# Routed experts of a mixer and MoE layer: gate and up products made transposed, weight loads split in two

## The reference

```python
def moe_ffn(h, w_router, router_bias, wg, wu, wd, sg, su, sd):
    xf = h.reshape(-1, d).astype(F32)
    idx, w = route(xf, w_router, router_bias)          # 6 of 64 experts for each token
    routed = routed_experts(xf, idx, w, wg, wu, wd)
    shared = (silu(xf @ sg) * (xf @ su)) @ sd
    return (routed + shared).reshape(bsz, seq, d)
# for the rows x of one expert e, each with its weight:
#   y = (silu(x @ wg[e]) * (x @ wu[e])) @ wd[e],   wg, wu: 1024 x 256,   wd: 256 x 1024
```

## Time and profile before

| what | us |
|---|---|
| runs (three) | 2062.09, 2062.33, 2065.42 |
| median | 2062.33 |
| profiled execution, span from first to last instruction | 2064.1 |
| of it: TensorE busy | 1995.9 |
| VectorE, GpSimd, ScalarE busy | 1138.1, 774.3, 504.3 |

### The profile page before, as it was taken

The page is one execution under the profiler, slowest core; times in us unless marked ns, Lnnn a source line. Parts: engine busy times, 40 slices in busy tenths (PEclk is TensorE's granted clock), DMA queues, the critical chain, the costliest instruction groups (busy, mean ns, idle before and its releaser), DMA issues.

```text
span 2064.1 us, 23702 instructions
## 1 busy us (share of the span) xinstructions
PE 1995.9 (97%) x7237; PEld 1014.8 (49%) x7238; DVE 1138.1 (55%) x3065; ACT 504.3 (24%) x1102; POOL 774.3 (38%) x717
## 2 busy tenths in 40 slices
PE   8999999999999999999999999999999999999991
PEld 6444667575544444444445554444444444444440
DVE  6222546776611222335676656966666666666645
ACT  3111554452322222214432230111111111111113
POOL 1762005612122222115980002554545545545531
PEclk9999999999999999999999999999999999999996
DMA  5421000011132222144253006999999999999974
GB/s 147 132 87 41 21 21 22 22 47 47 46 130 75 72 82 77 57 124 167 101 203 144 38 31 258 341 356 348 349 356 352 358 361 350 352 352 354 353 238 168
DMA packets 129639, 370.45 MB, mean 179 GB/s; under 512 B 33712, under 2 KB 65668, under 8 KB 103832
## 3 DMA queue, kind: packets, MB, share of 16 engines
q1 hardware_dynamic: 103960, 314.83, 40.8%
q0 software_dynamic: 23520, 54.61, 10.9%
q10 hardware_dynamic: 2080, 0.01, 0.1%
HBM read 320.57 MB, written 68.17 MB: 188 GB/s over the span
## 4 chain that ended last, share of the span: by engine, by line
PE 46%; POOL 3%; DVE 2%; issue 2%; DMA 1%; ACT 0%; SPq 0%; DVEq 0%; POOLq 0%
PE banks L3164 22%; PE banks L3180 10%; PE banks L2288 4%; PE banks L2335 3%; POOL arena L2136 2%; PE banks L2014 2%; PE banks L279 1%; PE banks L2351 1%; PE banks L2776 1%; PE banks L3172 1%; PE banks L2311 1%; DMA arena<-in_w_router_dram 0%; DVE arena L3240 0%; DVE arena L3157 0%; PE banks L2298 0%
## 5 line engine op out<-in xcount | busy, mean ns | idle before, releaser
L3164 PE MATMUL banks<-arena 128*128 128x512 f32 x1056 | 470.5, 598 | 3.1 <-DVE arena L3157 0.7
L3143 POOL DMA_INDIRECT arena<-h_rows,index x268 | 276.7, 1032 | 142.1 <-issue 73.6
L3164 PEld LDWEIGHTS banks<-arena 128*128 128x128 f32 x1056 | 195.8, 190 | 227.2 <-issue 225.8
L1720 PE MATMUL banks<-arena 128*128 128x512 f32 x672 | 299.0, 594 | 1.5 <-ACT arena L323 1.5
L3180 PE MATMUL banks<-arena 128*128 128x512 f32 x528 | 237.6, 592 | 1.3 <-ACT arena L2979 0.8
L3151 POOL DMA_INDIRECT sums<-arena,row_to x66 | 108.0, 1636 | 274.5 <-DMA sums<-arena,row_to 255.6
L3157 DVE STREAM_TRANSPOSE arena<-arena 128x1024 f32<-128x1024 f32 x66 | 133.9, 2028 | 134.3 <-PE banks L3164 134.3
L279 PE MATMUL banks<-arena 128*128 128x512 f32 x416 | 193.5, 602 | 2.2 <-PEq L108 2.2
L1720 PEld LDWEIGHTS banks<-arena 128*128 128x128 f32 x672 | 123.1, 190 | 136.1 <-issue 133.9
L3127 DVE TENSOR_SCALAR index<-row 32x1 uint32<-32x1 f32 x1072 | 155.4, 145 | 17.1
L3180 PEld LDWEIGHTS banks<-arena 128*128 128x128 f32 x528 | 100.2, 190 | 127.0 <-issue 125.3
(11 more groups left out here) (400 smaller groups left out, 2428.9 us busy)
## 6 DMA issues: line engine op xcount, KB each, us to landing
arena<-in_w_exp_gate_dram SPq DMA_DIRECT2D x66, 1024.0 KB, 9.1
arena<-in_w_exp_up_dram SPq DMA_DIRECT2D x66, 1024.0 KB, 11.2
arena<-in_w_exp_down_dram SPq DMA_DIRECT2D x66, 1024.0 KB, 18.1
arena<-in_w_in_dram SPq DMA_DIRECT2D x26, 1024.0 KB, 5.4
gates<-arena SPq DMA_DIRECT2D x60, 256.0 KB, 2.0
arena<-gates SPq DMA_DIRECT2D x15, 1024.0 KB, 7.6
arena<-h_rows,index POOLq DMA_INDIRECT x268, 7.9
arena<-in_x_dram SPq DMA_DIRECT2D x8, 512.0 KB, 5.6
```

Source lines behind the costliest of these rows:

```text
L1720: mm = pe.matmul(gate_bank(n, b), left[:, k, :], right[:, k, :], start=(alone and k == 0), stop=(k == 3), skip_group_check=True)
L3143: return pool.indirect_dma_start(w.x[k][:, 256 * q:256 * (q + 1)], None, rows, bass.IndirectOffsetOnAxis(ap=g.index[:, k, q:q + 1], axis=0 ...
L3164: mm = pe.matmul(g.bank[:, 2, :].rearrange("p (a f) -> p a f", a=2), xT[:, k, :], wgu[:, :, k, :], start=(k == 0), stop=(k == KT - 1))
```

## The change

Gate and up are made transposed: the weights become the stationary operand, 128 hidden features at a time, and the 128 rows the moving one. `up_products` then makes four blocks (gate and up, even and odd hidden features) in the four quarters of bank 2, each in 8 calls of 128 columns. The product of silu(gate) and up is then already what `turn_hid` made; `turn_hid`, its copy on ScalarE, `w.hid` and the semaphores hT and hTr go, and VectorE writes to one of two `w.hidT` by turns. The down planes get semaphores of their own (`exp_down_in`). `up` waits for gate and up (32), `down` for the down plane (16). SyncE asks for gate and up of block b+4 behind `up(b)`, and for the down plane of block b+4 behind `down(b)`.

```diff
 def up_products(g, pe, xT, slot):
     wgu, _ = expert_weights(g, slot)
-    for k in range(KT):
-        mm = pe.matmul(g.bank[:, 2, :].rearrange("p (a f) -> p a f", a=2), xT[:, k, :], wgu[:, :, k, :],
-                       start=(k == 0), stop=(k == KT - 1))
-    return mm
-
-
-def turn_hid(g, pe, hid):
-    cols = hid.rearrange("p (n k) -> p k n", k=2)
-    for k in range(2):
-        mm = pe.transpose(g.bank[:, 3, k * P:(k + 1) * P], cols[:, k, :], g.ident[:])
+    for a in range(2):
+        for f in range(2):
+            out = g.bank[:, 2, (2 * a + f) * P:(2 * a + f + 1) * P]
+            for k in range(KT):
+                cols = wgu[:, a, k, :].rearrange("p (n j) -> p j n", j=2)
+                mm = pe.matmul(out, cols[:, f, :], xT[:, k, :], start=(k == 0), stop=(k == KT - 1))
     return mm
...
+def load_gate_up(g, sp, e, slot, done=None):
+
+    done = done or g.exp_in[slot]
     at = RING[slot]
+    sp.dma_start(g.region(at, 2048), expert_plane(g, e, "w_exp_gate")).then_inc(done, 16)
+    sp.dma_start(g.region(at + 2048, 2048), expert_plane(g, e, "w_exp_up")).then_inc(done, 16)
+
+
+def load_down(g, sp, e, slot, done=None):
+
+    sp.dma_start(g.region(RING[slot] + 4096, 2048),
+                 expert_plane(g, e, "w_exp_down")).then_inc(done or g.exp_down_in[slot], 16)
...
         @block.sync
-            def load(i, c):
+            def load(i, c, next_up=True):
 
                 sp.wait_ge(s["down"], val(i, c) + 1)
-                load_expert(g, sp, val(i, c) + 4, c)
+                load_down(g, sp, val(i, c) + 4, c)
+                if next_up:
+                    sp.wait_ge(s["up"], val(i, c) + 2)
+                    load_gate_up(g, sp, val(i, c) + 5, (c + 1) % 4)
...
+            sp.wait_ge(s["up"], 1)
+            load_gate_up(g, sp, 4, 0)
...
             e = chosen_expert(sp, 0)
+            sp.wait_ge(s["up"], NE - 3)
+            load_gate_up(g, sp, e, 0)
             sp.wait_ge(s["down"], NE - 3)
-            load_expert(g, sp, e, 0)
+            load_down(g, sp, e, 0)
...
             def up(i, c):
                 pe.wait_ge(s["xT"], val(i, c) + 1)
-                pe.wait_ge(g.exp_in[c % 4], (quarter(i, c) + 1) * 48)
+                pe.wait_ge(g.exp_in[c % 4], (quarter(i, c) + 1) * 32)
                 wait(pe, s["hid"], val(i, c))
                 up_products(g, pe, w.xT, c % 4).then_inc(s["up"], 1)
 
-            def turn_hidden(i, c):
-                pe.wait_ge(s["hid"], val(i, c) + 1)
-                wait(pe, s["hTr"], val(i, c))
-                turn_hid(g, pe, w.hid).then_inc(s["hT"], 1)
-
             def down(i, c):
-                pe.wait_ge(s["hTr"], val(i, c) + 1)
+                pe.wait_ge(s["hid"], val(i, c) + 1)
                 wait(pe, s["ya"], val(i, c))
                 wait(pe, s["yb"], val(i, c))
+                pe.wait_ge(g.exp_down_in[c % 4], (quarter(i, c) + 1) * 16)
...
             def hidden(i, c):
                 dve.wait_ge(s["silu"], val(i, c) + 1)
-                wait(dve, s["hT"], val(i, c))
-                dve.tensor_tensor(w.hid, w.silu, bank[:, 2, FF:], ALU.mult).then_inc(s["hid"], 1)
+                if has(i, c, -2):
+                    dve.wait_ge(s["down"], val(i, c) - 1)
+                dve.tensor_tensor(w.hidT[c % 2].rearrange("p k n -> p (k n)"), w.silu, bank[:, 2, FF:],
+                                  ALU.mult).then_inc(s["hid"], 1)
...
-            def hidden(i, c):
-                act.wait_ge(s["hT"], val(i, c) + 1)
-                wait(act, s["down"], val(i, c))
-                act.activation(w.hidT.rearrange("p k n -> p (k n)"), bank[:, 3, 0:FF], ACT.Copy).then_inc(s["hTr"], 1)
```

More of the change, by code:

```diff
@@ L2226, in norm_and_route @@
     g.exp_in = [g.keep(f"exp_in{i}") for i in range(4)]
+    g.exp_down_in = [g.keep(f"exp_down_in{i}") for i in range(4)]
     flat2 = lambda a: bank[:, a:a + 2, :].rearrange("p b n -> p (b n)")
@@ L2662, in expert_weights, with expert_plane, load_expert @@
     return g.region(RING[i], 2, KT, FF), g.region(RING[i] + 4096, 2, D)
-def load_expert(g, sp, e, slot=None, sems=None):
-    slot = e % 4 if slot is None else slot
-    s = (sems or g.exp_in)[slot]
-    at = RING[slot]
[L2670 to L2673, removed]
+def expert_plane(g, e, name):
+    w = g.ins[name]
+    plane = w[0, e] if isinstance(e, int) else w[0, bass.ds(e, 1)].rearrange("a n f -> (a n) f")
+    return plane.rearrange("(p k) f -> p (k f)", p=P)
+def load_gate_up(g, sp, e, slot, done=None):
+    done = done or g.exp_in[slot]
+    at = RING[slot]
+    sp.dma_start(g.region(at, 2048), expert_plane(g, e, "w_exp_gate")).then_inc(done, 16)
[3 more added lines that the diff above has]
+                 expert_plane(g, e, "w_exp_down")).then_inc(done or g.exp_down_in[slot], 16)
+def load_expert(g, sp, e):
+    load_gate_up(g, sp, e, e)
+    load_down(g, sp, e, e)
 def experts(g):
@@ L2683, in experts @@
     first = norm_and_route(g, w, joint)
-    names = "q lst list flag row idx xT up silu hid hT hTr down ya yb to tables tabled places".split()
+    names = "q lst list flag row idx xT up silu hid down ya yb to tables tabled places".split()
     s = {n: sem("e_" + n) for n in names}
-    more = "places q lst list flag row idx xT up silu hid hT hTr down ya yb to gathered stored free used".split()
+    more = "places q lst list flag row idx xT up silu hid down ya yb to gathered stored free used".split()
     v = {n: sem("v_" + n) for n in more}
@@ L2748, in _ @@
                 sp.dma_start(dst, src.rearrange("(a n) -> a n", a=1).to_broadcast([P, D])).then_inc(g.gb_in, 16)
-            with sp.Fori(0, NE // 4 - 1) as i:
+            sp.wait_ge(s["up"], 1)
+            load_gate_up(g, sp, 4, 0)
+            with sp.Fori(0, NE // 4 - 2) as i:
                 for c in range(4):
                     load(i, c)
+            for c in range(4):
+                load(NE // 4 - 2, c, c < 3)
             e = chosen_expert(sp, 0)
+            sp.wait_ge(s["up"], NE - 3)
+            load_gate_up(g, sp, e, 0)
             sp.wait_ge(s["down"], NE - 3)
-            load_expert(g, sp, e, 0)
+            load_down(g, sp, e, 0)
             n = rest_count(sp)
@@ L2760, in _ @@
                 sp.wait_ge(v["used"], o + 1)
-                load_expert(g, sp, e, 1, {1: loaded})
+                load_gate_up(g, sp, e, 1, loaded)
+                load_down(g, sp, e, 1, loaded)
             last.sync(sp)
@@ L2808, in step @@
                     first.last_down()
-                turn_hidden(i, c)
             def ready():
@@ L2830, in _ @@
                 pe.wait_ge(v["hid"], o + 1)
-                turn_hid(g, pe, w.hid).then_inc(v["hT"], 1)
-                pe.wait_ge(v["hTr"], o + 1)
                 pe.wait_ge(v["ya"], o + 1)
                 pe.wait_ge(v["yb"], o + 1)
-                down_products(g, pe, w.hidT, 1).then_inc(v["down"], 1)
+                down_products(g, pe, w.hidT[1], 1).then_inc(v["down"], 1)
                 pe.matmul(bank[0:1, 0, 8:9], g.ident16[:, 0:1], g.ident16[:, 0:1],
@@ L2997, in step @@
                     result(i, c - 1)
-                hidden(i, c)
             count = []
@@ L3088, in expert_work @@
     w.q = take(NT * P // 2).bitcast(BF16).rearrange("p (m n) -> p m n", m=NT)
-    w.silu, w.hid, w.hidT = g.region(LISTS + 2048, FF), g.region(LISTS + 2048 + FF, FF), take(2, P)
+    w.silu = g.region(LISTS + 2048, FF)
+    w.hidT = [take(2, P), g.region(LISTS + 2048 + FF, 2, P)]
     g.over, g.ovend, g.ones64, g.iota48 = take(NE), take(NE), take(NE), take(48)
```

9 lines of the change are left out of this document (4 added, 5 removed).

## The result

| | runs | us, median (lowest to highest) |
|---|---|---|
| before, same chip | 4 | 2063.43 (2062.09 to 2065.42) |
| after | 4 | 2073.43 (2072.94 to 2074.66) |

The ratio is 1.0047, with a 95% interval of 1.0035 to 1.0059: the change costs 10 us. The profiled execution took 2074.66 us, its span 2072.9 us against 2064.1.

What follows compares the result with a forecast made beforehand. It took TensorE as the bound, transfers a close second. Per block +0.37 (up), -0.23 (turns), -0.26 (lists) over 62 blocks gave -7.4 us; with the tail -9.6, span 2054.5, so 2053 us, range 2048 to 2086.

Steps and rivals of the forecast that it cites:

- Up's pace: In up's 64 short products, weight loads set the pace: 0.113 us each, up 7.31 us, 0.37 more a block.
- rival B: In up, the column step costs a few ns a load: 2069 us at 0.117, 2085 at 0.121; chance 0.24.
- The cachelines: In up's loads, by the skill, two reads per 16-byte line keep full bandwidth: pace 0.112 us, up 7.25.
- Lists: The eight list products a block, no longer behind the wait for hid, fall from 0.47 to 0.21 us, saving 0.26.
- What is late next: At the next up's wait for hid and xT: ready 2.60 us behind up, needed at 3.64, so 1.0 us left.
- Transfers: In the expert stream, transfers need 11.24 us a block against 10.95, falling behind 18 us over 62 blocks; it barely fits.
- the floor: At block 64, the planes' landing near 1993 us limits the stream's gain to about 8.5 us; the forecast took 7.4.
- The tail: Behind the stream, two waits go: 1.2 us between turn and down of block 64, 1.0 us in the rest loop.
- C: In up, the step adds its full 56 ns to every load: pace 0.169 us, near 2275 us; chance 0.14.
- D: In TensorE's loop, the longer body no longer stays loaded, each of 14 returns costing about 1.88 us: 2079 us; chance 0.06.
- E: In each block the lists stay at 0.47 us: 2069 us at pace 0.113, 2065 at 0.112; chance 0.08.
- The split: In the weight loads, asking for gate and up earlier makes room for the transfers but by itself gains nothing.

Runs made afterwards that it cites:

- e8: The changed kernel with each up load's 128 columns at a step of four floats instead of two, so products mix columns: 2562.82 us (one run).
- e9: The changed kernel with each up load's 128 columns at a step of three floats instead of two, so products mix columns: 2309.7 us (one run).
- e1: The changed kernel with adjacent columns of gate and up as stationary blocks, the down plane loaded in two 4 KB runs to match: 2065.43 us, ratio 1.0006 to before.
- e3: The kernel before with its list products moved ahead of the turns, nothing else: 2065.18 us, ratio 1.0002 to before.
- e11: e1 with its three weight planes asked for together behind the down products: 2060.76 us, ratio 0.9991 to the kernel before.
- e6: e1 with the up plane bringing only 256 of 2048 floats a partition behind the fourth expert: 2050.1 us, ratio 0.9933 to the kernel before.
- e4: The kernel before with its loads split as in the change, nothing else: 2063.77 us, ratio 1.0001 to before.
- e5: The changed kernel with its three planes again asked for together behind the down products: 2073.13 us, ratio 1.0041 to the kernel before.
- e10: The changed kernel with the up plane bringing only 256 of 2048 floats a partition behind the fourth expert: 2075.42 us (one run).
- e12: The kernel before with both its lists behind the down products (e3) and its loads split (e4): 2065.33 us, ratio 1.0006 to before.
- e2: e1 with the down plane loaded as in the changed kernel, so hidden features meet wrong down rows: 2066.89 us, ratio 1.0012 to the kernel before.
- e7: e1 with odd experts' rows added into a second array, so a scatter waits for the one before the last: 2067.68 us, ratio 1.0013 to before.

## Why the prediction was wrong

It said 2053, faster; the truth is 2073.4, inside the range and on the other side. The mechanism was right, that in a row of short products the weight load sets the pace; the size of that load was not. By its own steps:

**Up's pace: the step that failed.** The prediction took 0.113 us a load, "near the row of ordinary loads". It is 0.1177, over the 0.1148 that it had named as the point from which rival B decides. 64 x 0.0047 = 0.30 us a block, 18.7 us over 62 blocks. That is nearly the whole distance from 2053 to 2073.4. The prediction had the rows for it. Its own warning was the 197 ns of the turns' loads against 190; it read them as standing "about where an ordinary float32 load stands already", but an added 6 or 7 ns on a load is what separates 0.112 from 0.118 once 64 loads stand in a row. The two turns showed it too, at the rounding of the rows: 0.23 us against 0.22. The first of their loads runs behind the products of down, so the 0.01 us is that of one load, of which the chain has 64.

**The cachelines.** e8, e9 and e1 give the law that was missing. 128 columns that span 2048, 1536 and 1024 bytes of a partition load in 0.233, 0.174 and 0.1177 us, 0.113 to 0.115 ns a byte; adjacent ones (512 bytes) in 0.112, where the same law would give an estimated 0.058. In these four points a float32 load takes the longer of its own 0.112 and the time to read the stretch it spans, and a step of two floats lies just over where the two meet. Bytes spanned and 16-byte lines touched are the same count up to a step of four (64, 96 and 128 lines, 1.81 to 1.84 ns a line); a wider step would tell them apart, and none was run. The Trainium skill (SBUF — State Buffer, the part on cachelines under "Door 1") asks for two reads in each 16-byte line; a step of four floats has one, and the pace falls from one load in 0.1177 us to one in 0.233, so the traces agree that such a step is not free. At two reads a line they show 0.1177 and not the 0.112 of adjacent columns: what the rule calls full bandwidth is 5% short here, and 5% was the question.

**Turns.** They are gone, 0.23 us a block, as forecast.

**Lists.** 0.26 of 0.26 us: 0.21 us are left. e3 shows the reason that was given, with nothing else changed: with their place ahead of the wait for hid the same eight products take 0.21 us in the kernel before. What the average did not say is that most of the 0.26 was paid in one block of four, at the loop's return.

**What is late next.** Nothing: hid is ready at 1362.26, the next up starts at 1363.30, 1.0 us later, as worked out.

**Transfers.** The kernel after never waits for them: 11.26 us a block against the estimate of 11.24. That estimate came out well; held blocks take 11.1 (e11), 11.3 (e3) and 11.4 us (e1) on average. The warning that "the stream cannot gain more than about 8.5 us, whatever TensorE does" was put to the test by e1, which has the 10.87 us a block of the forecast and better. It gained 8.0 us on the kernel after (2073.4 to 2065.4) and nothing on the one before. From about its 41st block on its blocks take 11.4 us on average (20 blocks from 1733.99 to 1962.05), and e6 shows that the transfers are behind it. So the forecast had a second error, which a right pace would have laid bare: it let the whole 7.4 us through the floor. With 10.95 us a block the real kernel would most likely have ended near e1; that is an estimate, as no run has that block. The prediction counted only what the ring of four places lends to the weights, and in e1 TensorE never waits for a plane. The scatters have less to lend: each waits for the one before it, and a result for the scatter two blocks back. They ran out first, from about the 40th block on.

**The tail.** Of 1.2 + 1.0 us the second came. The first did not, since the products wait for the banks to be read (1.22 us against 1.21): a wait that the turn had covered. And 3.5 us were saved at the end of the hardware loop, which no step had.

**The rivals.** B is what happened, near the lower end of its pace: 2069 was its time at 0.117, and 0.1177 adds 0.04 us a block to that, an estimated 2072. That it comes so near the 2073.4 is in part luck: the 3.5 us at the loop's end that went and the 2.5 us at the tail that did not come (1.2 and the two longer ups) nearly cancel. C is out as stated (0.169 us with a step of two), though a step of three does cost that much. D: the longer loop body is not loaded again; q8 has 49 packets in the whole run against 44 before, and TensorE is busy in every us of the three windows shown. E is out.

**The split.** e4 and e5: nothing in either kernel, as the prediction said of the split by itself. That it "is what makes that room" for a faster TensorE did not show either: e11, without it, is no slower than e1.

## What to carry to other kernels

Before a long product is cut into short ones, take the pace of a chain of such loads with the very access pattern, to the ns: when the load is what sets the pace, a price of 5% that hardly shows in a pair of transposes is paid in every one. And where a second resource stands at 1.00 beside the busy one, work out for how many blocks each chain of buffers can lend time, the results' as well as the weights'; if the stream is longer than that, a faster engine shows at first and gives most or all of it back (e1, e3). Fewer bytes gave it back here (e6), and another order of asking at most a part (e11). A wait ahead of register-addressed products also holds the preparing of those products, most of all where the loop returns; put them ahead of it (e3).

## What the runs showed of the hardware

- Float32 weight loads of 128 columns, 128 rows, in a row: 0.112 us adjacent, 0.1177 at a step of 8 bytes, 0.174 at 12, 0.233 at 16. Transfers beside them at 1.01 or 0.87 of the DMA engines make no difference (after, e10).
- At the end of the hardware loop TensorE loses 3.5 us in the kernel before (1.88 us idle, then an up 1.7 us longer), and nothing in the kernel after and e5. e3, e4 and e12 stand idle there for 2.2, 2.0 and 2.2 us; the longer up shows in e3 (8.67 us), whose loads are joint as before, and not in e4 and e12, whose loads are split (7.1 us). Packets of TensorE's instructions do not explain it: q8 has one behind the idle time before (1951 to 1962 us) and one after (1960 to 1970), and none from 1935 to 1970 us in e3, e4 and e12, which lose time there too. Why the kernels with 64 short products lose nothing was not tried.
- Single gaps of up to 0.7 us inside an up whose operands are all there, between its 42nd and 50th product, show in e1, e2 and e11. They do not show in e6, where the transfers are lighter, nor in e7, where the bytes are the same and no scatter waits for the last. What TensorE waits for there the profile does not say ("issue"); it stays open.
- In e1 and e2, once the results wait for scatters, ScalarE and VectorE, which wait for an up to end, start 1.2 to 2.4 us behind it in 20 blocks in a row and not 0.2 to 0.3. e6 and e7 have one such block each, e11 none. The cause stays open too.
- A load row of 190 ns is not its price in a row: loads overlap, and 192, 196, 261 and 329 ns of the rows (adjacent in e1, step of 2, 3, 4) go with 112, 118, 174 and 233 ns from start to start.
